# Order of the exponentials, the logs and the squares in the recurrence of a hybrid layer, with one weight split moved to GpSimd

## The reference, cut to what matters

```python
def forget_gate(f_logits, lb):
    f = lb + (1.0 - lb) * jax.nn.sigmoid(f_logits)
    return split_heads(jnp.log(f)), split_heads(1.0 - f)      # log f, and the keys k = 1 - f
...
def step(state, xs):                                          # gla_scan, chunk by chunk
    qc, kc, vc, gc = xs
    b = jnp.cumsum(gc, axis=2)
    b_last = b[:, :, -1:, :]
    k_dec = kc * jnp.exp(b_last - b)
    new_state = jnp.exp(b_last[:, :, 0, :, None]) * state + jnp.einsum('bhck,bhcv->bhkv', k_dec, vc)
    o_inter = jnp.einsum('bhtk,bhkv->bhtv', qc * jnp.exp(b), state)
    ...
    scores = jnp.einsum('bhtk,bhsk,bhtsk->bhts', qc, kc, decay)
    return new_state, o_inter + jnp.einsum('bhts,bhsv->bhtv', scores, vc)
...
y = o * lax.rsqrt(jnp.mean(o * o, axis=-1, keepdims=True) + EPS)   # hgrn_readout
return merge_heads(y) * norm_g * jax.nn.silu(g)
```

## Time and profile before

| | us |
|---|---|
| runs (three) | 2210.11, 2213.41, 2215.37; median 2213.41 |
| the profiled execution | 2215.54, its span 2213.8 |
| recurrence stage | about 535 to 937 of the span |
| mean granted TensorE clock | 0.977 of full speed |

### The profile page before, as it was taken

How to read it: one execution, slowest core, us unless ns; L and a number is a source line. 1 busy time by engine, 2 the same in 40 slices (tenths; PEclk the granted TensorE clock), 3 DMA queues, 4 the chain that set the end, 5 groups by cost and what they waited for, 6 DMA issues and landing times. The chain is left out here.

```text
span 2213.8 us, 37194 instructions
## 1 busy us (share of the span) xinstructions
PE 2069.9 (93%) x14088; PEld 1366.2 (62%) x14214; DVE 1591.3 (72%) x2253; ACT 960.3 (43%) x1320; POOL 443.9 (20%) x445
## 2 busy tenths in 40 slices
PE   5799999998999999899957999999999999999995
PEld 2344444433877787644417777777777777777772
DVE  3799999775778787866685666666666666666666
ACT  3610011545566656545433444444434444444344
POOL 2500001011556556300021110111111101110111
PEclk9899999999999999999978999999999999999998
DMA  9831003564020211399836888777778887877786
GB/s 334 172 85 38 20 29 99 165 192 148 6 58 22 77 59 25 135 267 280 233 143 238 248 245 267 247 252 236 251 247 252 249 257 247 256 240 248 242 278 263
DMA packets 338499, 407.06 MB, mean 184 GB/s; under 512 B 158575, under 2 KB 204175, under 8 KB 337897
## 3 DMA queue, kind: packets, MB, share of 16 engines
q1 hardware_dynamic: 320136, 346.47, 50.1%
q0 software_dynamic: 16224, 56.73, 8.7%
q10 hardware_dynamic: 2050, 2.70, 0.3%
HBM read 313.96 MB, written 62.54 MB: 170 GB/s over the span
## 5 line engine op out<-in xcount | busy, mean ns | idle before, releaser
L90 PE MATMUL pgu<-xlo,mwhi 128*128 128x256 bf16 x2048 | 558.4, 273 | 0.0
L89 PE MATMUL pgu<-xhi,mwhi 128*128 128x256 bf16 x2048 | 558.3, 273 | 0.0
L91 PE MATMUL pgu<-xhi,mwlo 128*128 128x256 bf16 x2048 | 558.3, 273 | 0.0
L2738 DVE TENSOR_TENSOR mwlo<-mwst,mwhi 128x2048 bf16<-128x2048 f32 x187 | 426.8, 2282 | 0.0
L2638 ACT ACTIVATE mwhi<-mwst 128x2048 bf16<-128x2048 f32 x186 | 350.8, 1901 | 12.8 <-DMA mwst<-in_w_gate 12.8
L2646 ACT ACTIVATE thb<-pgu 128x256 f32<-128x256 f32 x128 | 49.1, 384 | 541.4 <-PE pgu L91 541.4
L871 DVE SCALAR_TENSOR_TENSOR co<-u,taps,co 128x1984 f32<-128x1984 f32 (+22 forms) x120 | 234.1, 1951 | 3.7
L2749 DVE SCALAR_TENSOR_TENSOR thb<-thb,pgu 128x256 f32<-128x256 f32 x128 | 53.7, 420 | 245.0 <-ACT thb L2646 245.0
L89 PEld LDWEIGHTS pgu<-xhi,mwhi 128*128 128x128 bf16 x2048 | 200.4, 98 | 24.9
L90 PEld LDWEIGHTS pgu<-xlo,mwhi 128*128 128x128 bf16 x2048 | 200.4, 98 | 24.5
L91 PEld LDWEIGHTS pgu<-xhi,mwlo 128*128 128x128 bf16 x2048 | 200.4, 98 | 23.1
(11 more groups left out here) (405 smaller groups left out, 3956.8 us busy)
## 6 DMA issues: line engine op xcount, KB each, us to landing
mwst<-in_w_gate SPq DMA_DIRECT2D x32, 2048.0 KB, 9.3
mwst<-in_w_up SPq DMA_DIRECT2D x32, 2048.0 KB, 8.2
mwst<-in_w_down SPq DMA_DIRECT2D x32, 2048.0 KB, 11.4
wst<-in_w_in SPq DMA_DIRECT2D x28, 512.0 KB, 5.6
u<-in_ada_w SPq DMA_DIRECT2D x12, 1024.0 KB, 6.2
big<-in_ada_w SPq DMA_DIRECT2D x4, 2048.0 KB, 19.7
xt<-in_x SPq DMA_DIRECT2D x16, 512.0 KB, 6.2
s_y<-x SPq DMA_DIRECT2D x16, 512.0 KB, 6.6
```

The source lines that it names most:

```text
L89: nc.tensor.matmul(out, lh, rh, start=(first and k == 0), stop=False)
L90: nc.tensor.matmul(out, lh, rl, start=False, stop=False)
L91: ins = nc.tensor.matmul(out, ll, rh, start=False, stop=(last and k == n - 1))
L2738: nc.vector.tensor_tensor(wlo[:, b, ks], wst[:, b % NS, ks], whi[:, b, ks], ALU.subtract)\
```

## The change

Five edits in `heads_stage`:

1. `exps` makes the keys' factor first, exp(-B) into E, and then the queries' factor exp(B) over B. So `decay_k` reads E, and `decay_q`, `decay_q_start` and `score` use B. The waits follow: the logarithm into E waits for GpSimd's use of it two units before, the scan into B waits for the scores and for QI. The last head's read-out uses E where it used B as spare room.
2. `sums` takes middles and ends with two `tensor_reduce` (maximum over one element) in place of two copies.
3. ACT does `squares` after `logs` in its pass.
4. PE does `mean` after all of `output`, where it was between its two halves.
5. The low part of the forward gate weight is made on GpSimd (`forward_split`, pass 6, between `decay_k` and `normed`/`low`); DVE keeps the backward one.

```diff
-        lrs = [rsb[:, 0], rsb[:, 1], B[:, 0], B[:, 1]]
+        lrs = [rsb[:, 0], rsb[:, 1], E[:, 0], E[:, 1]]
...
-                    nc.gpsimd.tensor_tensor(diagonal(p, nt), b4(KK), b4(B), ALU.mult).then_inc(kh_ok, 1)
+                    nc.gpsimd.tensor_tensor(diagonal(p, nt), b4(KK), b4(E), ALU.mult).then_inc(kh_ok, 1)
...
+                def forward_split(h):
+                    wait(pool, w_hi, h * 2 + 1)
+                    nc.gpsimd.tensor_tensor(wlo[:, 0], wst[:, 0], whi[:, 0], ALU.subtract).then_inc(w_lo, 1)
...
                         if there(i + 1, prev, cur, nxt):
                             decay_k(h, i + 1)
+                        if nxt and i == 6:
+                            forward_split(h + 1)
...
-                    wait(act, at_ps, X(h, i - 1))
-                    wait(act, qi_ok, X(h, i - 1))
+                    wait(act, kh_ok, U(h, i - 1))
                     nc.scalar.activation(E[:, p, 0:n], KK[:, p, 0:n], ACT.Ln, bias=1.0, scale=-1.0).then_inc(lf_ok, 1)
...
                     wait(act, d_ok, U(h, i) + 1)
+                    nc.scalar.activation(E[:, p, 0:n], B[:, p, 0:n], ACT.Exp, scale=-1.0).then_inc(eb_ok, 1)
                     if real:
-                        nc.scalar.activation(E[:, p, 0:n], B[:, p, 0:n], ACT.Exp).then_inc(ee_ok, 1)
-                        wait(act, ee_ok, X(h, i) + 1)
-                    nc.scalar.activation(B[:, p, 0:n], B[:, p, 0:n], ACT.Exp, scale=-1.0).then_inc(eb_ok, 1)
+                        wait(act, eb_ok, U(h, i) + 1)
+                        nc.scalar.activation(B[:, p, 0:n], B[:, p, 0:n], ACT.Exp).then_inc(ee_ok, 1)
...
-                        for r, j in due(h, i, 9, prev, cur):
-                            squares(r, j if nxt or i < 9 else 1)
                         for r, j in due(h, i, 12, prev, cur):
                             cast(r, j)
                         if there(i + 2, prev, cur, nxt):
                             logs(h, i + 2)
+                        for r, j in due(h, i, 9, prev, cur):
+                            squares(r, j if nxt or i < 9 else 1)
...
                 def split(h, d):
                     wait(dve, w_hi, h * 2 + d + 1)
+                    wait(dve, w_lo, h * 2 + d)
...
                     wait(dve, lf_ok, U(h, i) + 1)
-                    wait(dve, kh_ok, U(h, i - 1))
+                    wait(dve, at_ps, X(h, i - 1))
+                    wait(dve, qi_ok, X(h, i - 1))
...
-                    nc.vector.tensor_copy(s3[:, :, 0:4], b4[:, :, :, mid]).then_inc(b_ok, 1)
-                    nc.vector.tensor_copy(s3[:, :, 8:9], b3[:, :, end:end + 1]).then_inc(b_ok, 1)
+                    nc.vector.tensor_reduce(s3[:, :, 0:4], b4[:, :, :, mid:mid + 1], AX.X, ALU.max).then_inc(b_ok, 1)
+                    nc.vector.tensor_reduce(s3[:, :, 8], b3[:, :, end:end + 1], AX.X, ALU.max).then_inc(b_ok, 1)
...
-                        if nxt and i in (6, 7):
-                            split(h + 1, i - 6)
+                        if nxt and i == 7:
+                            split(h + 1, 1)
...
                             if ahead and mm < ST:
                                 project(h, i + 3, ST + mm)
-                            if mm == ST - 1:
-                                for r, j in due(h, i, 9, prev, cur):
-                                    mean(r, j)
+                        for r, j in due(h, i, 9, prev, cur):
+                            mean(r, j)
```

More of the change, by code:

```diff
@@ L1526, in decay_q @@
                     wait(dve, q_in[s], h * 16 + 16)
-                    nc.vector.tensor_tensor(E[:, i % 2], qT[:, s * SEG:(s + 1) * SEG], E[:, i % 2], ALU.mult)\
+                    nc.vector.tensor_tensor(B[:, i % 2], qT[:, s * SEG:(s + 1) * SEG], B[:, i % 2], ALU.mult)\
                         .then_inc(qh_ok, 1)
@@ L1538, in decay_q_start @@
                     b4 = lambda t: t[:, p].rearrange("p (t b j) -> p t b j", b=BLK, j=CH)
-                    nc.vector.tensor_tensor(b4(QI), b4(E), se[:, p, :, 0:4].unsqueeze(3).broadcast_to([P, ST, BLK, CH]),
+                    nc.vector.tensor_tensor(b4(QI), b4(B), se[:, p, :, 0:4].unsqueeze(3).broadcast_to([P, ST, BLK, CH]),
                                             ALU.mult).then_inc(qi_ok, 1)
@@ L1722, in score @@
                     ins = nc.tensor.matmul(pat[0:keys, n * CH:(n + 1) * CH], KX[:, p, n * P:n * P + keys],
-                                           E[:, p, n * CH:(n + 1) * CH], start=True, stop=True)
+                                           B[:, p, n * CH:(n + 1) * CH], start=True, stop=True)
                     if n == ST * BLK - 1:
```

## The result

The changed kernel takes 2217.13 us (median of 20 runs, 2213.7 to 2221.93), the kernel before 2214.41 in the runs beside it (20 runs, 2210.11 to 2216.97). The ratio is 1.0014 with a 95% interval of 1.0008 to 1.0021: 3.1 us slower, by 1.8 to 4.6. The 3.1 is less than the 0.2% (4.4 us) that I set as the bound between "same" and "slower"; the upper end of the interval just reaches beyond it. Forecast were 2214.1 (0.7 above the median of the three runs of before) and a chance of 0.66 for "within 0.2%".

A forecast was written before the change was run, and what follows sets the result against it. PE bounds the recurrence, busy 373 of 402 us, so only its few waits count. Terms +3.1 +0.45 -0.66 -1.8 -0.8 +0.45 sum to +0.7 us, predicting 2214.1; range 2208.5 to 2219.

The forecast's parts named there:

- an exchange of waits on PE: Main case: PE's waits in the recurrence trade off, 2214.1 us, from 2210 to 2217.5; chance 0.56.
- The +0.7 in the middle: Sum of all terms over the whole kernel: +0.7 us, giving a predicted median of 2214.1.
- Squares and mean: Passes 1, 3, 5, heads 1 to 3: PE's mean waits for later squares; +3.1 us, plus +0.45 net through pass 1.
- Rival (c): Low part on GpSimd holds the scan, 2.2 us later in three heads; slower, 2219.3 us; chance 0.16.
- The keys' exp first: GpSimd's keys' product starts 0.66 sooner: -0.66 in the first head, -1.8 at pass 8's output, -0.8 in the tail.
- rival (b): GpSimd's products lead passes 6 to 8, so 0.66 returns at three DVE places; faster, 2207.9 us; chance 0.17.
- The tail: Last head: earlier GpSimd shortens the scan by 0.5 and the following `both`; -0.8 us, bounds 0 to -1.2.
- The low part: Pass 6: GpSimd takes 2.2 us for it, `low` then delays the subtraction; +0.15 a head, +0.45 in heads 0 to 2.
- Maxima: Reductions replace copies in `sums`; the subtraction takes over the copy's wait in pass 1; gain on PE taken as 0.
- Rival (d): Reductions lift the wait from the whole group before unit 3's scores; at most -1.9, 2211.5 us; chance 0.04.
- the sign that I had named for this: Profile after: maxima of 0.18 with a subtraction over 1.2 in pass 1 would confirm the reductions' zero gain.
- The credit of pass 2: Mean's delay of 1.34 in pass 1 set against the existing wait for unit 3's scores; net +0.15 a head.

The follow-up runs named there:

- run 11: Changed kernel plus 11 spare matmuls in PE's wait of pass 1 and 9 in that of pass 8; 0.9985 of the kernel before.
- run 8: Changed kernel plus 11 spare matmuls before PE's wait for the squares of pass 1; 0.9998 of the kernel before.
- run 10: Changed kernel with squares before logs, both low parts on DVE, plus 4 spare matmuls in pass 1 and 9 in pass 8; 0.9954 of the kernel before.
- run 4: Kernel before with only the order of the exps changed, keys' exp first into E; 0.9969 of the kernel before, 6.9 us below.
- run 6: Kernel before with only the two copies of middles and ends made reductions; 0.9992 of the kernel before, zero inside the interval.
- run 3: Kernel before with only the squares moved behind the logs and the mean behind the output; 1.0017 of the kernel before, 3.8 us above.
- run 1: Changed kernel with squares and mean back in their old places; 0.9966 of the kernel before, 7.5 us below.

## Why the prediction was right, and where its terms were off

The forecast (no change within 0.2%, an exchange of waits on PE) holds, and 2217.13 lies in the range. The +0.7 in the middle doesn't hold: the runs give +3.1, and not less than 1.8. That it came as near as it did is partly luck. Of the 3.9 us by which the stage grew, 3.35 are the lower clock in passes 1 and 2 and 1.0 is the lower clock in pass 8. Without them the waits come to -0.4, where the sum has +0.7: its terms for passes 6 to 8 were too small a gain by 1.5, the others together too small a cost by 0.3, and the clock, for which it has no term, outweighed both. In its parts:

- **Squares and mean.** Predicted +0.51 in each of passes 3 and 5, +1.34 at the mean of pass 1, +0.15 net at the scores of unit 3. Pass 5 measured +0.53 in all three heads, pass 1 +1.53 and +1.43 where the clock is full, passes 1 to 3 with the score's wait +0.73, +0.77 and +0.56 against 0.66. Together 3.65 against 3.55. The sequence of steps was right, and the total to a tenth.
- **What the sum left out: the clock.** The row of 2.38 in pass 8 was there before. I read that wait as a place where time could be had back, not as one that can slow what follows. In pass 1 the new wait of 2.4 us costs 2.4 us less what it replaces and hides, and then in some executions another 1.7. Run 11 against the changed kernel (6.4 us), and the clock in the waits that runs 8, 10 and 11 fill, show it as a cause; the sum has no term for it. Rival (c) had the sign but another mechanism, and its 2.2 per head at the scan didn't occur (the scan of pass 6 takes 1.46 in the changed kernel).
- **The keys' exp first.** Predicted -0.66 in head 0 at unit 2, measured -0.38; -0.6 a head in passes 7 and 8, measured alone -1.6 in head 1 and -0.9 in head 0 (run 4), since `both` of pass 6 gains like that of pass 7. The step that failed is the reading of PE's waits: the list had no wait in pass 7, and the row of 703.70 has one of 0.59, which this gain reaches. Here rival (b) had the mechanism right at two of its three places and was about two thirds true; at the third, the scan of pass 7, nothing changed (2.29 in both). The tail was -0.8 as predicted, but as a remainder: -1.64 at the last scores, of which 0.8 is lost again further on. Both executions had stretches at the lower clock there, and what takes the 0.8 isn't shown.
- **The low part.** Predicted +0.15 a head, measured +0.8 alone and +0.34 beside the new exps. The duration was right (2.13 against 2.2); I had let the exps' 0.66 pay for `low`, and it pays for less of it.
- **Passes 6 to 8 together.** Predicted -1.35 over heads 0 to 2, measured -1.9, which looks close. But 1.0 of clock is in the -1.9; the waits alone gave -2.9.
- **Maxima.** Predicted 0, measured within 0.3 a head in either direction; the wait goes to the subtraction. Rival (d) is refuted by the 1.30 of its row in run 6. In pass 1 of the changed kernel the sign that I had named for this, a subtraction over 1.2, isn't there (0.69): with the read-out later, the scan ahead of it has the wait (2.12, last section).
- **The credit of pass 2.** I set the wait for the scores of unit 3 against the mean's delay. That gave the right total and hid that two edits compete for the same microsecond: the exps' order alone is worth 6.9 us, the squares' order takes it all back and 3 more. A prediction by parts would have shown which edit to drop.

That the mean's wait comes before the scores' wait and fills it is measured only through run 3 against run 1. Why the clock falls behind some of the waits and not others stays open.

## What to carry to other kernels

When one in-order engine is busy without a break, look only at its few waits, and ask of each edit which of them it fills or opens; a helper moved by half a microsecond in a stretch without waits costs it in full. Two edits that aim at one wait can't both have it, so price each alone as well as together. And a wait on TensorE of some 2.4 us, as here, can have a second price in the clock of the matmuls behind it, which spare matmuls in the wait avoid without shortening it. What that price comes to depends on what stands behind: 1.7 us where the matmuls run on without a wait, 0 to 0.8 where one follows that the slower work fills.

## What the runs showed of the hardware that I had not expected

- In the eleven profiled runs and those of the two kernels, PE waited 2.0 us or more 31 times in passes 1 and 8 of the stage, and 18 stretches at the lower granted clock came with them, which began between 0.8 us before the wait's end and 1.5 us behind it; between 28 us from the stage's start and its tail there was none without such a wait. Of the waits before the mean of pass 1, 6 of 9 had one, of those in pass 8, 12 of 22. In the ten places where such a wait was filled with spare matmuls (runs 8, 10 and 11) there was none. One such stretch costs 1.7 us in passes 1 and 2 (8.33 us of work took 9.98; 0.83 and 0.87 on two neighbouring distances).
- Where the waits were filled (run 11) the clock stayed at 1.00 over 340 us.
- The lower clock comes in some executions and not in others, in changing passes. That may be part of the spread over 20 runs each (8.2 us from lowest to highest for the changed kernel, 6.9 for the kernel before); the mean clocks of the runs differ, but no run here separates this from other causes.
- A GpSimd instruction and a DVE instruction can hold each other up even where both have begun: a DVE scan that takes 1.23 us where it begins first lasted 2.12 in pass 1 behind a GpSimd product of 1.26 that had begun 0.23 before it. In the kernel before it was the other way round: there this product began 0.04 behind the scan (646.11) and lasted 2.26. GpSimd's row of the changed kernel, then DVE's:

```profile
639.76 1.26 POOL L1315 TENSOR_TENSOR of<-of,rsb 128x512 f32<-128x512 f32 x1
```

```profile
639.99 2.12 DVE L1506 TENSOR_TENSOR_SCAN B<-segm,E 128x512 f32<-128x512 f32 x1 [2.84 <-ACT E L1368]
```
